# Start addresses of TensorE's operands in SBUF: streamed operands at 192 bytes past a multiple of 256, stationary ones at a multiple of 256

## The chip, the core and the metric

One core of one Trainium2 chip. The metric is device time in microseconds (us) for one execution of the whole program; the kernel before takes 1875.76 us (median of 3 runs, 1871.45 to 1876.39).

## The reference

Two blocks on 256 tokens of width 1024, all in float32. The first block has two layers; each layer is a gated feed-forward (width 2816), a mixer (a gated spatial unit beside differential attention, merged by gates), and another gated feed-forward, each followed by a layer norm:

```python
h = _swiglu(x, ffn_w1[l, 0], ffn_w3[l, 0], ffn_w2[l, 0])
x = _layernorm(ALPHA * x + 0.5 * h, ln_g[l, 0], ln_b[l, 0])
h = _mixer(x, l, w_in[l], gate_b[l], ...)
x = _layernorm(ALPHA * x + h, ln_g[l, 1], ln_b[l, 1])
h = _swiglu(x, ffn_w1[l, 1], ffn_w3[l, 1], ffn_w2[l, 1])
x = _layernorm(ALPHA * x + 0.5 * h, ln_g[l, 2], ln_b[l, 2])
```

The second block has one layer: neighbourhood attention and gated linear attention side by side, gates, an output projection, and a last gated feed-forward. Nearly all arithmetic is in the products of the activations with the weight matrices.

## The kernel before

**Products in three parts.** A weight matrix comes from HBM in chunks of 1 MB into one of three buffers `raw`. A chunk is cut into parts of 128 x 1024 numbers. For each part ScalarE writes a rounded copy `whi` (line 1371) and VectorE the remainder `wlo` (line 1835; a few times GpSimd), in four buffers of each, used in turn (`n % 4`). Activations are kept in the same two pieces, as `XTh` and `XTl`, `HCh` and `HCl`, or `ffn1Hh` and `ffn1Hl`. A product is then three matmuls: high by high, high by low, low by high.

**Two forms.** TensorE holds one operand in the array (the stationary one, 128 x 128, loaded by an LDWEIGHTS of its own for each matmul) and streams the other past it.
- `gemm_a` (lines 685, 686, 688): the weights stand, the activations stream, 256 columns. A part gives 8 x 3 = 24 matmuls. Used by all `ffn_up` stages (44 parts, 1056 matmuls each), by the mixer's q, k, u and gate projections (40 parts, 960 matmuls a layer), by its two branch projections (16 parts, 384 matmuls a layer), and by most of the second block.
- `gemm_b` (lines 708, 710, 711): the activations stand, the weights stream, 512 columns. Used by `ffn_down` (264 matmuls each), by the mixer's v, val and out projections (96 each), and by parts of the second block.

**Order.** Each engine runs a list written out by hand; they meet only through semaphores. TensorE goes through the stages in the order of the reference. Between the weight parts of the mixer, small matmuls are put in: a permutation after each q or k part (line 867), and attention steps after each gate part. In `ffn_up` up to two short modulation steps (lines 766, 768, 786) are put in. After each stage of the first block a layer norm turns the activations into `XTh` and `XTl` (TensorE line 746, ScalarE line 1379, VectorE line 1844).

**Where the operands begin.** A partition of SBUF holds the buffers one after another, so each start follows from the sizes. All of `raw`, `whi` and `wlo` begin at multiples of 512 bytes. `HCh` and `HCl` begin at a multiple of 256. The buffers of `XT` and of the feed-forward's hidden values are 512 bytes larger than needed, and the offset at which they are used differs by stage (in bytes, for the high and the low piece; the rooms themselves begin at multiples of 512):

```python
X_AT = ((256, 256), (128, 128), (64, 64), (192, 192), (384, 384), (64, 320))
H_AT = ((256, 256), (128, 128), (64, 64), (256, 0), (448, 448))
```

`X_AT` goes by stage: entries 0 and 3 are the first `ffn_up` of layers 0 and 1, entries 1 and 4 their mixers, entries 2 and 5 their second `ffn_up`. `H_AT` goes by feed-forward: four in the first block, where the hidden values stand in `ffn_down`, and the last one in the second block (`ffn4`), where they stream through `gemm_a`. So within one execution the same loops run over operands at different offsets:

| stage | us from start | streams | stands | streamed begins past 256 | standing begins past 256 |
|---|---|---|---|---|---|
| ffn_up 0 | 11 to 143 | XT | weights | 0 | 0 |
| ffn_up 1 | 486 to 614 | XT | weights | 64 | 0 |
| ffn_up 2 | 688 to 816 | XT | weights | 192 | 0 |
| ffn_up 3 | 1162 to 1290 | XT | weights | 64 | 0 |
| mixers, q k u gates | 239 to 403, 915 to 1079 | XT | weights | 128 | 0 |
| mixers, branches | 403 to 451, 1079 to 1127 | HC | weights | 0 | 0 |
| ffn_down 0, 1, 2, 3 | 143, 615, 817, 1291 | weights | hidden | 0 | 0, 128, 64, 0 |
| mixers, v, val, out | 218, 319, 452 and on | weights | XT | 0 | 128 |
| second block, forms a | 1500 to 1683 | HC | weights | 0 | 0 |
| last ffn_up | 1683 to 1803 | HC | weights | 0 | 0 |
| last ffn_down | 1803 to 1860 | hidden | weights | 192 | 0 |

**Small buffers that the change touches.** `csil` (64 bytes a partition) lies before `HCh`. In the second block `ones` is a matrix of ones for a column sum (line 1285), filled by GpSimd at line 2511; `rb` holds the reciprocal root of the last norm; `nm` is a mask that GpSimd reads at lines 2549 and 2552 for the attention bias; `c2` is a table of the linear attention.

Of the kernel before, what the change touches and what calls it, by code (L numbers as in the profile page):

```python
# [9 lines left out]
F32R = mybir.dt.float32r  # L10
# [4 lines left out]
D = 1024  # L15
T = 256
# [257 lines left out]
X_AT = ((256, 256), (128, 128), (64, 64), (192, 192), (384, 384), (64, 320))  # L274
H_AT = ((256, 256), (128, 128), (64, 64), (256, 0), (448, 448))
# [79 lines left out]
def program(nc, I, out):  # L355
# [5 lines left out]
    def shifted(stack, name, n):  # L361

        room = sb(stack, name, [128, n * T + 128], F32R)
        return lambda by: room[:, by // 4:by // 4 + n * T].rearrange("p (k c) -> p k c", k=n)
# [7 lines left out]
    with ctx:  # L372
# [27 lines left out]
        whi = some(ctx, "whi", 4, [128, 1024], F32R)  # L400
        wlo = some(ctx, "wlo", 4, [128, 1024], F32R)
# [3 lines left out]
        csil = sb(ctx, "csil", [128, 8, 2])  # L405
# [4 lines left out]
        sh = sb(ctx, "sh", [128, 48, 2])  # L410
        g1c = sb(ctx, "g1c", [128, 8, 2])
# [3 lines left out]
        sb(ctx, "gap0", [128, 80])  # L415
# [8 lines left out]
        XH, XL = [room_h(h) for h, _ in X_AT], [room_l(l) for _, l in X_AT]  # L424
# [8 lines left out]
        def ffn_bufs(st, name, *at):  # L433
            hh, hl = shifted(st, name + "Hh", NF), shifted(st, name + "Hl", NF)
            S, Hf = some(st, name + "S", 2, [128, T]), some(st, name + "Hf", 2, [128, T])
            return [(hh(h), hl(l), S, Hf) for h, l in at]


        with ExitStack() as st:
            ffn1 = ffn_bufs(st, "ffn1", *H_AT[0:3])  # L440
# [23 lines left out]
        with ExitStack() as st:  # L464
            ffn3 = ffn_bufs(st, "ffn3", H_AT[3])
# [5 lines left out]
        ones = sb(st, "ones", [128, 128])  # L471
        rb = sb(st, "rb", [128, T])
# [6 lines left out]
        nm = sb(st, "nm", [128, 2, 64])  # L479
        OGh, OGl = HCh[:, 0:4, T:512], HCl[:, 0:4, T:512]  # L480
# [26 lines left out]
        with ExitStack() as fs:  # L507
            sb(fs, "gap2", [128, 128])
            ffn4 = ffn_bufs(fs, "ffn4", H_AT[4])
            OUT = sb(fs, "OUT", [128, 2, D])  # L510
        st.close()
        FFN = [*ffn1, *ffn3, *ffn4]
# [13 lines left out]
        def hi_part(n):  # L526
            a, b = chunks[parts[n][0]][3][parts[n][1]][2:]
            return whi[n % 4][:, 0:a * b].rearrange("p (k c) -> p k c", k=a)

        def lo_part(n):  # L530
            a, b = chunks[parts[n][0]][3][parts[n][1]][2:]
            return wlo[n % 4][:, 0:a * b].rearrange("p (k c) -> p k c", k=a)
# [134 lines left out]
        def tensor(e):  # L667
# [66 lines left out]
            def xt(s):  # L734
                return lambda k: (XH[s][:, k, :], XL[s][:, k, :])

            def xt_b(s):
                return lambda k, t: (XH[s][:, k, t * 128:(t + 1) * 128], XL[s][:, k, t * 128:(t + 1) * 128])
# [103 lines left out]
            def mixer(l):  # L842
# [16 lines left out]
                gemm_b(("V", l), 8, 1, xt_b(s), (0, 1), [[4, 5], [6, 7]], 1024, lambda k, t: ready(k, (t,)), tail=3, between=turn_ws)  # L859
# [11 lines left out]
                for n in range(16):  # L871
                    b = n % 4
                    empty(b)
                    gemm_a(bank[b][:, 0:T], xt(s), ("qk", l, n), ready=ready if n == 0 else None)
# [14 lines left out]
                for n in range(8):  # L889
                    b = n % 4  # L890
                    empty(b)
                    gemm_a(bank[b][:, 0:T], xt(s), ("u", l, n))
# [3 lines left out]
                gemm_b(("val", l), 8, 1, xt_b(s), (0, 1), [[4, 5], [6, 7]], 1024, tail=2)  # L896
# [51 lines left out]
                for n in range(16):  # L948
                    b = n % 3
                    empty(b)  # L950
                    gemm_a(bank[b][:, 0:T], xt(s), ("gate", l, n))
# [24 lines left out]
                gemm_b(("out", l), 8, 1, xt_b(s), (0, 1), [[4, 5], [6, 7]], 1024, m_ready)  # L976
# [21 lines left out]
            def second():  # L998
# [281 lines left out]
                def add_square(k):  # L1280
# [4 lines left out]
                    e.matmul(bank[5][:, 0:T], ones[:, :], tmp[t2r.slot["sq", k]][:, :], start=k == 0, stop=k == 7).then_inc(  # L1285
# [63 lines left out]
            for l in range(2):  # L1349
# [3 lines left out]
                ffn_up(2 * l, xt(3 * l), x_ready(3 * l), at)  # L1353
# [4 lines left out]
                ffn_up(2 * l + 1, xt(3 * l + 2), x_ready(3 * l + 2), ffn_mods(2 * l + 1))  # L1358
# [5 lines left out]
        def scalar(e):  # L1364
# [10 lines left out]
            def turn_x(s, t):  # L1375
                for c in range(2):
                    b = (0, 1, 2, 0)[2 * t + c]
                    q.wait_ge(TURN, ("x", s, t, c))
                    e.activation(XH[s][:, 4 * c:4 * c + 4, t * 128:(t + 1) * 128], bank[b][:, :].rearrange("p (k c) -> p k c", k=4),
# [63 lines left out]
            def mixer(l):  # L1443
# [97 lines left out]
                for n in range(8):  # L1541
                    w.pass_by(1)
                    if n:
                        high("m", XH[3 * l + 1], n - 1, mtmp[tm[l].slot["m", n - 1]], ("m", l, n - 1))
                high("m", XH[3 * l + 1], 7, mtmp[tm[l].slot["m", 7]], ("m", l, 7))
# [23 lines left out]
            def second():  # L1569
# [214 lines left out]
                e.activation(rb[:, :], rb[:, :], ACTF.Sqrt).then_inc(A2.did("root"), 1)  # L1784
# [42 lines left out]
        def vector(e):  # L1827
# [11 lines left out]
            def turn_x(s, t):  # L1839
                for c in range(2):  # L1840
                    b = (0, 1, 2, 0)[2 * t + c]
                    hi = XH[s][:, 4 * c:4 * c + 4, t * 128:(t + 1) * 128]
                    q.wait_ge(XHI, ("x", s, t, c))
                    e.tensor_tensor(XL[s][:, 4 * c:4 * c + 4, t * 128:(t + 1) * 128], bank[b][:, :].rearrange("p (k c) -> p k c", k=4),  # L1844
# [72 lines left out]
            def mixer(l):  # L1917
# [122 lines left out]
                for n in range(8):  # L2040
# [6 lines left out]
                    if n:  # L2047
                        low("m", XL[3 * l + 1], XH[3 * l + 1], n - 1, mtmp[tm[l].slot["m", n - 1]])
                low("m", XL[3 * l + 1], XH[3 * l + 1], 7, mtmp[tm[l].slot["m", 7]])
# [47 lines left out]
            def second():  # L2097
# [232 lines left out]
                e.tensor_scalar(rb[:, :], bank[5][:, 0:T], 1.0 / D, RMS_EPS, ALU.mult, ALU.add).then_inc(D2.did("ms"), 1)  # L2330
                q.wait_ge(A2, "root")
                e.reciprocal(rb[:, :], rb[:, :]).then_inc(D2.did("rb"), 1)
# [315 lines left out]
```

## Time and profile before

| | |
|---|---|
| runs | 1871.45, 1875.76, 1876.39 us |
| the profiled execution | 1871.84 us, of which the span from first to last instruction is 1870.1 us |
| granted TensorE clock, mean | 0.994 of 2.4 GHz |
| TensorE matmuls | 1841.4 us busy, 98% of the span, 12859 instructions |
| TensorE weight loads | 1651.1 us, 88% |
| VectorE, ScalarE, GpSimd | 60%, 48%, 13% |
| DMA | 330.58 MB, mean 177 GB/s |

Matmuls overlap: one lasts longer than the distance to the start of the next. The time that a row of matmuls takes is therefore the number of them times the spacing of their starts. In a stretch without interruption the spacing is the length of the window, plus the duration of one matmul that overlaps its edges, over the count.

### The profile page before, as it was taken

Reading aid. Unit: us, or ns where it says so; the run is one execution under the profiler, and the core shown is the slowest. Engines: PE = TensorE matmul, PEld = TensorE weight load, DVE = VectorE, ACT = ScalarE, POOL = GpSimd, SP = SyncE. Lnnn points to the kernel's source line nnn. Section 1 sums busy time; section 2 is a strip of 40 time slices with the busy share of each in tenths; the row PEclk is TensorE's granted clock in tenths of the full one; section 3 lists DMA queues with packets and bytes.
Section 4 is the critical chain, followed back from the end, with each engine's and each line's share of the span. In section 5 each row is a group of like instructions: output and inputs, shape, how many; then the busy total and the mean of one; then the engine's idle time right before and its main releaser. Section 6 shows DMA issues by size and latency. Waiting matters only on the chain.

```text
span 1870.1 us, 31147 instructions
## 1 busy us (share of the span) xinstructions
PE 1841.4 (98%) x12859; PEld 1651.1 (88%) x12859; DVE 1125.8 (60%) x1703; ACT 890.3 (48%) x1437; POOL 245.6 (13%) x261
## 2 busy tenths in 40 slices
PE   9999999999999999999999999999998999999999
PEld 8998799999899879986898997999776787879999
DVE  5554676676656466655675776565653645565553
ACT  5544344664455435543435653555344345444443
POOL 1000232111200020001221212000111712100000
PEclk9999999999999999999999999999998999999999
DMA  8565654445666566764745455665444223356553
GB/s 277 187 203 192 232 187 155 162 136 183 203 192 211 196 209 182 243 207 157 251 158 180 136 170 191 226 209 185 170 129 131 90 77 105 113 160 191 186 182 117
DMA packets 252397, 330.58 MB, mean 177 GB/s; under 512 B 13162, under 2 KB 213072, under 8 KB 252256
## 3 DMA queue, kind: packets, MB, share of 16 engines
q1 hardware_dynamic: 248240, 315.31, 51.8%
q0 software_dynamic: 4016, 13.27, 2.0%
q8 instruction: 102, 1.67, 0.4%
q14 instruction: 39, 0.32, 0.1%
HBM read 327.51 MB, written 1.05 MB: 176 GB/s over the span
## 4 chain that ended last, share of the span: by engine, by line
PE 67%; issue 23%; DVE 5%; POOL 2%; ACT 2%; SPq 1%; DMA 1%; DVEq 0%; POOLq 0%; ACTq 0%
PE bank L685 15%; PE bank L688 15%; PE bank L686 15%; PE bank L708 5%; PE bank L710 5%; PE bank L711 5%; DVE X L1907 1%; DVE wlo L1835 1%; PE bank L1241 1%; SPq L654 1%; DMA raw<-in_w_in_dram 1%; ACT whi L1371 1%; POOL rs L2430 1%; PE bank L1219 1%; PE bank L867 1%
## 5 line engine op out<-in xcount | busy, mean ns | idle before, releaser
L1835 DVE TENSOR_TENSOR wlo<-raw,whi 128x1024 fp32r<-128x1024 f32 (+1 forms) x557 | 688.0, 1241 | 418.3 <-ACT whi L1371 415.2
L1371 ACT ACTIVATE whi<-raw 128x1024 fp32r<-128x1024 f32 (+1 forms) x569 | 594.4, 1051 | 425.3 <-PE bank L688 178.9
L685 PE MATMUL bank<-XTh,whi 128*128 128x256 f32 x2048 | 583.3, 285 | 2.8 <-DVE XTl L1844 2.8
L688 PE MATMUL bank<-XTh,wlo 128*128 128x256 f32 x2048 | 573.9, 280 | 0.0
L686 PE MATMUL bank<-XTl,whi 128*128 128x256 f32 x2048 | 573.7, 280 | 0.0
L685 PEld LDWEIGHTS bank<-XTh,whi 128*128 128x128 f32 x2048 | 386.1, 189 | 7.9 <-DVE XTl L1844 3.5
L686 PEld LDWEIGHTS bank<-XTl,whi 128*128 128x128 f32 x2048 | 386.4, 189 | 1.4
L688 PEld LDWEIGHTS bank<-XTh,wlo 128*128 128x128 f32 x2048 | 386.3, 189 | 0.0
L685 PE MATMUL bank<-HCh,whi 128*128 128x256 f32 (+1 forms) x936 | 274.1, 293 | 8.0 <-ACT whi L1371 5.9
L688 PE MATMUL bank<-HCh,wlo 128*128 128x256 f32 (+1 forms) x936 | 269.1, 287 | 0.0
L686 PE MATMUL bank<-HCl,whi 128*128 128x256 f32 (+1 forms) x936 | 269.0, 287 | 0.0
L685 PEld LDWEIGHTS bank<-HCh,whi 128*128 128x128 f32 x936 | 179.8, 192 | 26.3 <-issue 12.3
L688 PEld LDWEIGHTS bank<-HCh,wlo 128*128 128x128 f32 x936 | 179.6, 192 | 2.7 <-DVE wlo L1835 0.8
L686 PEld LDWEIGHTS bank<-HCl,whi 128*128 128x128 f32 x936 | 179.7, 192 | 2.1
L2430 POOL TENSOR_TENSOR rs<-rs,half 128x1 f32<-128x1 f32 x12 | 18.3, 1525 | 668.7 <-DVE rs L1901 668.7
L710 PE MATMUL bank<-wlo,ffn1Hh 128*128 128x512 f32 x264 | 103.8, 393 | 0.0
L708 PE MATMUL bank<-whi,ffn1Hh 128*128 128x512 f32 x264 | 103.8, 393 | 0.0
L711 PE MATMUL bank<-whi,ffn1Hl 128*128 128x512 f32 x264 | 103.7, 393 | 0.0
L708 PE MATMUL bank<-whi,XTh 128*128 128x512 f32 x192 | 77.2, 402 | 0.0
L711 PE MATMUL bank<-whi,XTl 128*128 128x512 f32 x192 | 77.1, 402 | 0.0
L710 PE MATMUL bank<-wlo,XTh 128*128 128x512 f32 x192 | 77.0, 401 | 0.0
L1403 ACT ACTIVATE ffn1S<-bank 128x256 f32<-128x256 f32 x66 | 25.4, 384 | 72.4 <-PE bank L688 72.4
(329 smaller groups left out, 2338.3 us busy)
## 6 DMA issues: line engine op xcount, KB each, us to landing
raw<-in_ffn_w_dram SPq DMA_DIRECT2D x131, 1024.0 KB, 5.1
raw<-in_w_in_dram SPq DMA_DIRECT2D x76, 1024.0 KB, 5.0
raw<-in_w_mod_dram SPq DMA_DIRECT2D x24, 1024.0 KB, 5.1
raw<-in_w_branch_dram SPq DMA_DIRECT2D x16, 1024.0 KB, 5.0
raw<-in_w_out_dram SPq DMA_DIRECT2D x12, 1024.0 KB, 5.0
raw<-in_w_ffn_gate_dram SPq DMA_DIRECT2D x11, 1024.0 KB, 5.1
raw<-in_w_ffn_up_dram SPq DMA_DIRECT2D x11, 1024.0 KB, 5.1
raw<-in_w_ffn_down_dram SPq DMA_DIRECT2D x8, 1024.0 KB, 5.0
```

Source lines behind the costliest of these rows:

```text
L654: e.dma_start(BT[64 * j:64 * j + 64, h, :, :], src).then_inc(BIAS[h].did(h, by=16), 16)
L685: e.matmul(o, hi[:, k, w0:w0 + nc_], xh, start=first and k == 0, stop=False)
L686: e.matmul(o, hi[:, k, w0:w0 + nc_], xl, start=False, stop=False)
L688: m = e.matmul(o, lo[:, k, w0:w0 + nc_], xh, start=False, stop=last and k == nk - 1)
L708: e.matmul(o[:, :], xh, hi[:, k, s], start=kk == 0, stop=False)
L710: e.matmul(o[:, :], xh, lo[:, k, s], start=False, stop=False)
L711: m = e.matmul(o[:, :], xl, hi[:, k, s], start=False, stop=kk == nparts * nk - 1)
L867: e.matmul(bank[b][:, 0:T], perm, mtmp[tm[l].slot["s", n]][:, :], start=True, stop=True).then_inc(SMALL.did(("perm", l, n)), 1)
L1371: e.activation(hi_part(n), raw_part(n), ACTF.Copy).then_inc(WHI.did(n), 1)
L1403: e.activation(S[s][:, :], bank[b][:, 0:T], ACTF.Silu).then_inc(AFF.did(("s", i, k)), 1)
L1835: e.tensor_tensor(lo_part(n), raw_part(n), hi_part(n).bitcast(F32), ALU.subtract).then_inc(WLO.did(n), 1)
L2430: e.tensor_tensor(rs[:, t, 1:2], rs[:, t, 0:1], nhalf, ALU.pow).then_inc(PLN.did(("rs", j, t)), 1)
```

## The change

Every operand of `gemm_a` and `gemm_b` that streams begins at 192 bytes (`MOVES`, 48 numbers) past a multiple of 256: `XT` in all stages, `HC` (by moving the 64 bytes of `csil` from before it to behind), the hidden values of the last feed-forward, and the weights `whi` and `wlo` in parts of 512 columns or more. Hidden values of the first block, the merged values `MX` of the mixer, and the weights in narrower parts begin at a multiple of 256 (`STANDS`). The buffers of `whi` and `wlo` grow by 256 bytes each, so the second and the fourth of each begin at 256 past a multiple of 512. `XT` as the stationary operand of the v and val projections, and `HC` as that of the second block, stay at 192. To make room, `ones` is laid over `nm` and `rb` over `c2`; the fill of `ones` on GpSimd moves behind the last use of `nm`, with a wait for it.

```diff
-X_AT = ((256, 256), (128, 128), (64, 64), (192, 192), (384, 384), (64, 320))
-H_AT = ((256, 256), (128, 128), (64, 64), (256, 0), (448, 448))
+MOVES, STANDS = 48, 0
...
-        whi = some(ctx, "whi", 4, [128, 1024], F32R)
-        wlo = some(ctx, "wlo", 4, [128, 1024], F32R)
+        whi = some(ctx, "whi", 4, [128, 1024 + 64], F32R)
+        wlo = some(ctx, "wlo", 4, [128, 1024 + 64], F32R)
...
-        csil = sb(ctx, "csil", [128, 8, 2])
         HCh = sb(ctx, "HCh", [128, 8, 512], F32R)
         HCl = sb(ctx, "HCl", [128, 8, 512], F32R)
...
+        csil = sb(ctx, "csil", [128, 8, 2])
...
-        XH, XL = [room_h(h) for h, _ in X_AT], [room_l(l) for _, l in X_AT]
+        XTh, XTl, MXh, MXl = room_h(MOVES), room_l(MOVES), room_h(STANDS), room_l(STANDS)
...
-            ffn1 = ffn_bufs(st, "ffn1", *H_AT[0:3])
+            ffn1 = ffn_bufs(st, "ffn1")
...
-            ffn3 = ffn_bufs(st, "ffn3", H_AT[3])
+            ffn3 = ffn_bufs(st, "ffn3")
...
-        ones = sb(st, "ones", [128, 128])
-        rb = sb(st, "rb", [128, T])
+        rb = c2[:, 0:T]
...
+        ones = nm[:, :, :].rearrange("p a c -> p (a c)")
...
-            ffn4 = ffn_bufs(fs, "ffn4", H_AT[4])
+            ffn4 = ffn_bufs(fs, "ffn4", MOVES)
...
         def hi_part(n):
             a, b = chunks[parts[n][0]][3][parts[n][1]][2:]
-            return whi[n % 4][:, 0:a * b].rearrange("p (k c) -> p k c", k=a)
+            at = MOVES if b >= 512 else STANDS
+            return whi[n % 4][:, at:at + a * b].rearrange("p (k c) -> p k c", k=a)
...
-                e.memset(ones[:, :], 1.0).then_inc(P2.did("ones"), 1)
...
+                q.wait_ge(P2, ("bias", 7))
+                e.memset(ones, 1.0).then_inc(P2.did("ones"), 1)
```

`lo_part` changes as `hi_part` does. No instruction is added or removed, and no shape changes.

## Rows read from the trace of the kernel before

**Rows 1.** The page: busy time of each engine; TensorE's granted clock in 40 slices.

```profile
PE 1841.4 (98%) x12859; PEld 1651.1 (88%) x12859; DVE 1125.8 (60%) x1703; ACT 890.3 (48%) x1437; POOL 245.6 (13%) x261
PEclk9999999999999999999999999999998999999999
```

**Rows 2.** Waits of TensorE: line, releaser, us in total, times, longest.

```profile
PE bank L685 <- ACT whi L1371: 5.9, 1, 5.9
PE bank L710 <- DVE wlo L1835: 4.0, 2, 3.3
```

**Rows 3.** Windows in three ffn_up stages: length, matmul busy (count), clock, DMA share, GB/s.

```profile
20.00:56.00 36.00, 36.00 (x303) 1.00 0.67 214
500.00:536.00 36.00, 36.00 (x308) 1.00 0.57 177
700.00:736.00 36.00, 36.00 (x320) 1.00 0.60 183
```

**Rows 4.** Line 686 in two of them: ns min/median/max, first and last start.

```profile
L686 PE MATMUL bank<-XTl,whi x101: 283/283/283, 19.9 to 55.9; 128*128 128x256 f32 x101
L686 PE MATMUL bank<-XTl,whi x106: 276/276/276, 700.0 to 735.7; 128*128 128x256 f32 x106
```

**Rows 5.** The same in the mixer, its branches and the last ffn_up.

```profile
L686 PE MATMUL bank<-XTl,whi x189: 274/281/287, 239.9 to 318.7; 128*128 128x256 f32 x189
L686 PE MATMUL bank<-HCl,whi x126: 278/283/283, 403.2 to 450.8; 128*128 128x256 f32 x126
L686 PE MATMUL bank<-HCl,whi x101: 283/283/283, 1699.9 to 1735.9; 128*128 128x256 f32 x101
```

**Rows 6.** The same in two stretches of the last ffn_down.

```profile
L686 PE MATMUL bank<-ffn4Hl,whi x35: 281/281/281, 1825.8 to 1837.8; 128*128 128x256 f32 x35
L686 PE MATMUL bank<-ffn4Hl,whi x37: 276/276/276, 1841.8 to 1854.0; 128*128 128x256 f32 x37
```

**Rows 7.** Windows in two ffn_down stages, columns as in Rows 3.

```profile
150.00:200.00 50.00, 50.00 (x222) 1.00 0.59 201
820.00:870.00 50.00, 50.00 (x216) 1.00 0.57 190
```

**Rows 8.** Line 711 in ffn_down 0, the val projection and ffn_down 2.

```profile
L711 PE MATMUL bank<-whi,ffn1Hl x74: 389/389/389, 149.7 to 199.4; 128*128 128x512 f32 x74
L711 PE MATMUL bank<-whi,XTl x18: 390/393/404, 323.9 to 335.8; 128*128 128x512 f32 x18
L711 PE MATMUL bank<-whi,ffn1Hl x72: 393/396/398, 820.0 to 869.7; 128*128 128x512 f32 x72
```

**Rows 9.** Groups of matmuls by shape: one of each form's three lines.

```profile
L686 PE MATMUL bank<-XTl,whi 128*128 128x256 f32 x2048 | 573.7, 280 | 0.0
L686 PE MATMUL bank<-HCl,whi 128*128 128x256 f32 x912 | 257.9, 283 | 0.0
L686 PE MATMUL bank<-ffn4Hl,whi 128*128 128x256 f32 x176 | 49.0, 278 | 0.0
L711 PE MATMUL bank<-whi,ffn1Hl 128*128 128x512 f32 x264 | 103.7, 393 | 0.0
L711 PE MATMUL bank<-whi,XTl 128*128 128x512 f32 x192 | 77.1, 402 | 0.0
L711 PE MATMUL bank<-whi,HCl 128*128 128x512 f32 x112 | 44.5, 397 | 0.0
L711 PE MATMUL bank<-whi,ffn3Hl 128*128 128x512 f32 x88 | 34.3, 390 | 0.0
```

**Rows 10.** VectorE's writes of XTl ahead of ffn_up 0 and of ffn_up 2.

```profile
L1844 DVE TENSOR_TENSOR XTl<-bank,XTh x4: 681/682/693, 7.4 to 10.6; 128x512 fp32r<-128x512 f32 x4
L1844 DVE TENSOR_TENSOR XTl<-bank,XTh x4: 681/684/693, 685.0 to 687.1; 128x512 fp32r<-128x512 f32 x4
```

**Rows 11.** Timeline of GpSimd: start, us; the fill of ones, and line 2558.

```profile
1392.18 0.22 POOL L2511 MEMSET ones<- 128x128 f32 x1
1497.21 0.72 POOL L2558 TENSOR_TENSOR ATG<-spare 128x256 f32<-128x256 f32 x1 [0.97 <-DVE spare L2208]
```

More of the change, by code:

```diff
@@ L361, in shifted @@
     def shifted(stack, name, n):
-        room = sb(stack, name, [128, n * T + 128], F32R)
-        return lambda by: room[:, by // 4:by // 4 + n * T].rearrange("p (k c) -> p k c", k=n)
+        room = sb(stack, name, [128, n * T + 64], F32R)
+        return lambda by: room[:, by:by + n * T].rearrange("p (k c) -> p k c", k=n)
     def some(stack, name, n, shape, dt=F32):
@@ L431, in program, with ffn_bufs @@
         cm, cos, sin, perm = csa[:, 0:256], csa[:, 256:512], csa[:, 512:768], csa[:, 768:896]
[L433 to L436, printed above, removed]
+        def ffn_bufs(st, name, at=STANDS):
+            return (shifted(st, name + "Hh", NF)(at), shifted(st, name + "Hl", NF)(at),
+                    some(st, name + "S", 2, [128, T]), some(st, name + "Hf", 2, [128, T]))
         with ExitStack() as st:
-            ffn1 = ffn_bufs(st, "ffn1", *H_AT[0:3])
+            ffn1 = ffn_bufs(st, "ffn1")
         with ExitStack() as st:
@@ L732, in gemm_b, with xt, xt_b, mx_b @@
                         between()
[L734 to L738, printed above, removed]
+            def xt(k):
+                return XTh[:, k, :], XTl[:, k, :]
+            def xt_b(k, t):
+                return XTh[:, k, t * 128:(t + 1) * 128], XTl[:, k, t * 128:(t + 1) * 128]
+            def mx_b(k, t):
+                return MXh[:, k, t * 128:(t + 1) * 128], MXl[:, k, t * 128:(t + 1) * 128]
             def turn_x(s, t):
@@ L895, in mixer @@
                         rotate(15)
-                gemm_b(("val", l), 8, 1, xt_b(s), (0, 1), [[4, 5], [6, 7]], 1024, tail=2)
+                gemm_b(("val", l), 8, 1, xt_b, (0, 1), [[4, 5], [6, 7]], 1024, tail=2)
                 for b in range(4, 8):
@@ L975, in m_ready @@
                     q.wait_ge(XLO, ("m", l, k))
-                gemm_b(("out", l), 8, 1, xt_b(s), (0, 1), [[4, 5], [6, 7]], 1024, m_ready)
+                gemm_b(("out", l), 8, 1, mx_b, (0, 1), [[4, 5], [6, 7]], 1024, m_ready)
             def context():
@@ L1284, in add_square @@
                         empty(5)
-                    e.matmul(bank[5][:, 0:T], ones[:, :], tmp[t2r.slot["sq", k]][:, :], start=k == 0, stop=k == 7).then_inc(
+                    e.matmul(bank[5][:, 0:T], ones, tmp[t2r.slot["sq", k]][:, :], start=k == 0, stop=k == 7).then_inc(
                         SMALL.did(("sq", k)), 1)
@@ L1352, in tensor @@
                     at[6] = turn_rows
-                ffn_up(2 * l, xt(3 * l), x_ready(3 * l), at)
+                ffn_up(2 * l, xt, x_ready(3 * l), at)
                 ffn_down(2 * l)
@@ L1357, in tensor @@
                 layernorm(3 * l + 1, (2, 8)[l])
-                ffn_up(2 * l + 1, xt(3 * l + 2), x_ready(3 * l + 2), ffn_mods(2 * l + 1))
+                ffn_up(2 * l + 1, xt, x_ready(3 * l + 2), ffn_mods(2 * l + 1))
                 ffn_down(2 * l + 1, context() if l else None)
```

38 lines of the change are left out of this document (19 added, 19 removed).

## The prediction

> **What bounds the kernel now.** The page first: TensorE's matmuls are busy for 98% of the span, the next engine for 60%, and the granted clock is at its upper level of 2.4 GHz nearly throughout [rows 1]. Then the waits: the longest that TensorE has for a split weight come to 5.9 and 4.0 us [rows 2]. So the time is a count of matmuls times the spacing of their starts, and an edit that touches only addresses can act only through that spacing. The kernel happens to run the same loop at different start offsets, so its own trace holds the comparison. ffn_up 0, 1 and 2 do the same work with the streamed activations 0, 64 and 192 bytes past a multiple of 256. In windows of 36 us they start 303, 308 and 320 matmuls [rows 3]. With one duration for the edges that is (36 + 0.283)/303 = 119.7, 117.8 and 113.4 ns each; I take 120.0 for the first, from its rows of starts. Streaming 256 columns at 2.4 GHz takes 106.7 ns, so 13.3 ns of loss at offset 0 have become 6.7 ns at 192. The duration of one follows: 283 ns at the first, 276 at the third, every one of them alike [rows 4]. Duration less 163 ns is the spacing, and I use that where interruptions spoil a count.
>
> **Form a, part by part** (counts are three times those of [rows 9], by stage as the loops give them).
> - ffn_up 0: 1056 matmuls from 120.0 to 113.4 ns: 7.0 us. ffn_up 1 and 3: 2112 from 117.8 to 113.4: 9.3 us. ffn_up 2 is at 192 already: 0. The last ffn_up, at offset 0, lasts 283 ns each, so 120 [rows 5]: 1056 by 6.6 is 7.0 us. These run with few interruptions, as ffn_up 2 does, and its rows are the price.
> - Stages with many interruptions have a second price. The last ffn_down streams at 192 too, and one of its stretches has 281 ns (118 ns apart), another 276 (113 apart), each of them constant, with four transposes between [rows 6]. So at 192 TensorE can fall into a slower rhythm and keep it until the next interruption. Bounds for the mixers and the second block are 113.4 and 117.8. I take 114.5, one restart in four slow, since ffn_up 2 comes back to 276 after its own. The mixers' q, k, u and gates stream at offset 128 with a median of 281 but a scatter of 274 to 287 [rows 5]; the distances of their starts average 118.8: 1920 by 4.3 is 8.3 us (1.9 to 10.4). Their branches are at 283, so 120 [rows 5]: 768 by 5.5 is 4.2 us (1.7 to 5.1). The rest of the second block, 912 matmuls: 5.0 us (2.0 to 6.0).
> - The last ffn_down keeps offset and rhythm: 0, give or take 1.
> Form a comes to 40.8 us, with 28.9 and 44.8 as ends.
>
> **Form b** has never streamed at anything but offset 0 in this trace; only the standing operand moved. ffn_down 0, both at 0: 222 starts in 50 us, (50 + 0.389)/222 = 226.9 ns, which is 213.3 for 512 columns plus 13.6; ffn_down 2, standing at 64: 216, or 233.3 ns [rows 7]. The durations agree, 389 and 396; the val projection, standing at 128, has a median of 393 and reaches 404 [rows 8], 232.4 ns on average. The price of streaming at 192 is thus unknown, and bounded by rows. The low end is 220: form a loses 13.3 ns at offset 0, form b 13.6, the same loss though it streams twice as long, and form a's shrinks by 6.6 at 192. The high end is 233.3: at standing 64 and streaming 0 the streamed operand begins 192 ahead of the standing one modulo 256, exactly the distance that the change makes. I take 220, for that equality of the two losses says that they arise in the same first part of a matmul, while the weights load. Counts again by [rows 9]:
> - ffn_down 0 and 3, 528 by 6.7: 3.6 us. ffn_down 1 (standing at 128, 232.4): 264 by 12.4, 3.3 us. ffn_down 2: 264 by 13.3, 3.5 us. out, where MX stands at 0: 192 by 12.4, 2.4 us.
> - v and val: XT stands at 192 and the weights stream at 192. Equal offsets exist only as 0 and 0, so 226.7 (220 to 233): 384 by 5.7, 2.2 us. HC in the second block goes from equal to equal, 0 (gain of 2.3 to loss of 2.2).
> Form b comes to 15.0 us, with a gain of 19.8 and a loss of 1.7 as ends.
>
> **The rest.** The writers' cost does not hang on the offset: VectorE writes XTl in 682 ns at offset 0 and in 684 at 192 [rows 10]. The modulation's 80 matmuls also stream at 192, under 1 us either way. Feeding: ffn_up 2 already ran at the new spacing with DMA at 183 GB/s in a window in which ffn_up 0 drew 214 [rows 3], and without a wait that lists among the longest [rows 2], so splits and loads can follow in the other stages. The fill of ones (0.22 us) moves behind GpSimd's last bias step, with a wait for its own predecessor. Queued behind it is line 2558, which sat idle for 0.97 us waiting for VectorE [rows 11]: that idle time covers it, and without it the sums for the linear attention, and TensorE behind them, would be those 0.22 us and the wait later. The reader of ones, line 1285, comes stages later. rb over c2 costs nothing: c2 has long been read.
>
> **A rule against it.** The rows show 120 and 113.4 ns for the same instruction at two addresses [rows 3]. The Trainium skill, TensorE: Matmul & The Clock Gate, Back-to-back issue gap, gives a gap that depends on the columns alone, and SBUF — State Buffer, Who interferes with whom, gives TensorE two independent read ports for the two operands. By both there is nothing to gain. The trace disagrees with the first by its number; of the second it shows only that the weight load and the stream together lose more or less by address. That result is rival 3 below.
>
> **The sum.** 40.8 + 15.0 = 55.8 us off the profiled execution of 1871.8 gives 1816.0. That execution is 3.9 us under the median of the runs, so I forecast 1820.
>
> **The rivals.**
> 1. *Only the distance between the two start offsets counts.* Then form b gets 233.3 in ffn_down and out: 528 by +6.6, 264 by +0.9 and 192 by +0.9 are a loss of 3.9, v and val still gain 2.2. For it: form b's worst row has this distance. Against it: the equal losses above. Gain 40.8 - 1.7 = 39.1: 1837.
> 2. *The slow rhythm is the rule.* The buffers' new stride or the restarts put TensorE at 118 in all of form a, ffn_up 2 with it: 2.3 + 0 + 2.3 + 5.6 - 4.6 = 5.6, and form b 4.4 above 220 where it streams at 192 against 0, 15.0 - 5.5 = 9.5. Total 15: 1861. For it [rows 6], against it the whole of ffn_up 2.
> 3. *The address is not the cause*, and ffn_up 2 is faster for some other reason of its own, so the change does not do what it says: 1876. Against it: three offsets, three spacings, and 281 or 276 only where the offset is 192.
> 4. *Slower.* Two of four standing weight buffers now begin at 256 past a multiple of 512. If the read pattern repeats over 512 bytes on the standing side, every second part meets a conflict. The price by form b's worst loss, 20 ns over the stream, is 106.7 + 20 = 126.7 for half of form a's 9408 matmuls, mean 120.0 against 118.2 now: +17, less 6 from form b at an unchanged 226.7, 1887. It decides from about 124 ns in the odd buffers. Against it: ffn_down 0 stands at 256 past 512 and ffn_down 3's low piece at 0, with 389 and 390 ns [rows 8, 9].
>
> **How the numbers follow.** Forecast 0.48, rival 1 0.33, rival 2 0.10, rival 3 0.05, rival 4 0.04. The predicted time is the forecast's, 1820. The forecast's own range, from the ends of the unknown prices, is 1811 (gain 65) to 1849 (gain 27), and holds rival 1. With some room for the scatter of the runs I give 1808 to 1850. About 0.3% is what a measurement can tell from no change: faster 0.92, same 0.04, slower 0.04.
>
> **What would show it.** Right: line 686 at 276 ns in every ffn_up, a 36 us window with 320 matmuls; line 711 at about 382 in ffn_down. Rival 1 shows as 396 there, rival 2 as 281 in line 686 over whole stages, rival 4 as two durations that alternate with the weight buffer. The prediction is wrong if TensorE's waits for `whi` or `wlo` grow past some 20 us, or if the mixers stay at 281.

## The result, and the profile after

| | before | after |
|---|---|---|
| runs, us | 1871.45, 1872.81, 1875.76, 1876.39 | 1837.98, 1841.89, 1842.32, 1847.04 |
| median | 1874.28 | 1842.11 |
| ratio | | 0.983, 95% interval 0.9802 to 0.9859 |
| profiled execution, its span | 1871.8, 1870.1 | 1842.3, 1840.6 |

A fourth run of the kernel before, 1872.81 us, came with the result and moves its median to 1874.28. The change takes 32 us off; 55.8 were forecast. The profiled executions differ by 29.5 us, in the span as in the time. The page of after, then its waits of TensorE (line, releaser, us in total, times, longest):

```profile
PE 1807.9 (98%) x12859; PEld 1615.1 (88%) x12859; DVE 1123.9 (61%) x1703; ACT 891.9 (48%) x1437; POOL 247.1 (13%) x261
PEclk9999999999999999999999999999998999999999
```

```profile
PE bank L684 <- ACT whi L1373: 6.2, 1, 6.2
PE bank L709 <- DVE wlo L1837: 4.1, 2, 3.4
```

The same number of matmuls, TensorE as full as before, and the two longest waits as they were [rows 1, 2]: splits and loads did follow, and nothing took TensorE's place as the bound. The gain is in the spacing. Windows of after in ffn_up 0, ffn_up 1, the last ffn_up, ffn_down 0 and ffn_down 2 (length, matmul busy and count, clock, DMA share, GB/s):

```profile
20.00:56.00 36.00, 36.00 (x319) 1.00 0.74 239
500.00:536.00 36.00, 36.00 (x320) 1.00 0.58 178
1690.00:1726.00 36.00, 36.00 (x320) 1.00 0.59 184
145.00:190.00 45.00, 45.00 (x195) 1.00 0.55 187
815.00:860.00 45.00, 45.00 (x194) 1.00 0.55 189
```

Where [rows 3] had 303 and 308 matmuls in 36 us there are now 319 and 320, that is 113.4 ns each, in every ffn_up. ffn_down has (45 + 0.396)/194.5 = 233.4 ns in both stages, where [rows 7] gave 226.9 for ffn_down 0. The matmuls themselves (lines are one lower than before in `gemm_a` and `gemm_b`; ns min/median/max): line 685 in ffn_up 0, the mixer's q, k, u parts, its gate parts, the neighbourhood attention and the last ffn_up, then line 710 in ffn_down 0 and the val projection.

```profile
L685 PE MATMUL bank<-XTl,whi x106: 276/276/279, 19.8 to 55.7; 128*128 128x256 f32 x106
L685 PE MATMUL bank<-XTl,whi x175: 276/281/282, 239.6 to 312.2; 128*128 128x256 f32 x175
L685 PE MATMUL bank<-XTl,whi x109: 276/276/282, 340.0 to 391.9; 128*128 128x256 f32 x109
L685 PE MATMUL bank<-HCl,whi x180: 276/281/281, 1479.8 to 1599.1; 128*128 128x256 f32 x180
L685 PE MATMUL bank<-HCl,whi x107: 276/276/276, 1679.8 to 1715.9; 128*128 128x256 f32 x107
...
L710 PE MATMUL bank<-whi,ffn1Hl x65: 393/393/398, 145.1 to 189.9; 128*128 128x512 f32 x65
L710 PE MATMUL bank<-whi,XTl x12: 389/389/389, 323.8 to 331.3; 128*128 128x512 f32 x12
```

Two durations, 276 and 281, now make up nearly all of form a (113.3 and 117.8 ns apart), where [rows 4, 5] had 283 and a scatter round 281. The long stretches have 276, the fast rhythm; the q, k, u parts and the attention have a median of 281, the slow one. In form b ffn_down lost its 389 [rows 8], and val got 389 for 393. The groups of line 685 and 710:

```profile
L685 PE MATMUL bank<-XTl,whi 128*128 128x256 f32 x2048 | 567.2, 277 | 0.0
L685 PE MATMUL bank<-HCl,whi 128*128 128x256 f32 x912 | 253.5, 278 | 0.0
L710 PE MATMUL bank<-whi,ffn1Hl 128*128 128x512 f32 x264 | 104.4, 395 | 0.0
L710 PE MATMUL bank<-whi,XTl 128*128 128x512 f32 x192 | 75.1, 391 | 0.0
```

Against [rows 9], form a is 3 to 5 ns shorter each, ffn_down 2 ns longer, and the projections from XT 11 ns shorter. Of these 11, some 7 are no effect of the addresses: in before's profile the first matmuls of both v projections were granted the lower clock of 1.2 GHz and last 628 ns, in after's profile none of them. Windows of before at the two places (columns as above):

```profile
214.60:218.00 3.40, 3.40 (x10) 0.51 1.02 416
890.50:893.90 3.40, 3.40 (x10) 0.50 1.03 414
```

In the stretches without interruption v and val went from 232.4 to 226.7, and out from 232.4 to 233.3.

**Where the 29.5 us are.** The length of each stage, from the start of its first to that of its last matmul of that form in the two traces, with the forecast beside it (us, gain positive; the second block's form a with HC stands in two stretches, and the row of its form b holds the first of them too):

| stages | length before | after | gain | forecast |
|---|---|---|---|---|
| ffn_up 0 | 131.7 | 124.7 | 6.9 | 7.0 |
| ffn_up 1 and 3 | 129.3, 129.3 | 124.6, 124.6 | 9.3 | 9.3 |
| ffn_up 2 | 129.5 | 129.5 | 0.0 | 0 |
| last ffn_up | 128.3 | 121.5 | 6.8 | 7.0 |
| mixers, q k u gates | 80.1, 60.8, 80.3, 60.8 | 79.3, 59.9, 79.3, 59.8 | 3.8 | 8.3 |
| mixers, branches | 48.6, 48.6 | 46.7, 46.7 | 3.8 | 4.2 |
| second block, other forms a | 5.6, 165.2 | 5.5, 165.1 | 0.2 | 5.0 |
| last ffn_down (to 1865.5 in before) | 62.0 | 62.0 | 0.0 | 0 |
| ffn_down 0 and 3 | 59.6, 61.6 | 61.4, 63.1 | -3.2 | 3.6 |
| ffn_down 1 | 61.1 | 61.4 | -0.3 | 3.3 |
| ffn_down 2 | 61.4 | 61.4 | 0.0 | 3.5 |
| out | 22.1, 22.1 | 22.2, 22.2 | -0.2 | 2.4 |
| v and val | 24.6, 22.1, 24.6, 22.1 | 23.9, 21.6, 23.5, 21.6 | 2.9 | 2.2 |
| HC, form b | 140.8 | 141.4 | -0.7 | 0 |

The gains sum to 29.3; the rest is rounding and the gaps between stages. Of the 26.5 us that the forecast had too much, 16.5 are form b (15.0 against -1.5) and 10 are form a (40.8 against 30.8), nearly all of these in the mixers and the second block.

Two rows hold the clock beside the addresses. In v the lower clock cost before's profile some 1.5 us at the start of each projection (the first ten intervals take 3.98 us, against 2.42 and 2.41 in after); 2.2 of these 3.1 us were not missed, as the one long pause in each was 1.0 us in before and 2.3 and 1.9 in after, so that some 0.9 of the 2.9 us are not the change's. In the second block the same 72 matmuls of form b with HC took 21.6 us in before and 22.9 in after, at equal spacing but with more of the stretch at the lower clock (window, matmul busy and count, clock, DMA share, GB/s; before, then after):

```profile
1451.50:1473.10 21.60, 18.25 (x74) 0.92 0.37 109
1427.80:1450.70 22.90, 19.52 (x73) 0.85 0.35 106
```

That row's loss of 0.7 is thus no sign of a price of the new addresses.

### The profile page after: what moved, and what is told of

It is laid out like the page before. It is cut to its first block, busy times and chain, and to the rows that moved or that the text cites. A ratio compares the mean times of both kernels' runs of the same rounds, so it can differ in the third digit from the quotient of the medians.

```text
span 1840.6 us, 31147 instructions
## 1 busy us (share of the span) xinstructions
PE 1807.9 (98%) x12859; PEld 1615.1 (88%) x12859; DVE 1123.9 (61%) x1703; ACT 891.9 (48%) x1437; POOL 247.1 (13%) x261
## 4 chain that ended last, share of the span: by engine, by line
PE 63%; issue 23%; DVE 6%; DMA 3%; POOL 2%; ACT 2%; SPq 1%; DVEq 0%; POOLq 0%; ACTq 0%
PE bank L684 15%; PE bank L687 14%; PE bank L685 14%; PE bank L707 4%; PE bank L709 4%; PE bank L710 4%; DMA G<-in_lam_dram 1%; DVE X L1909 1%; DVE wlo L1837 1%; PE bank L1243 1%; SPq L653 1%; DMA raw<-in_w_in_dram 1%; POOL rs L2432 1%; ACT whi L1373 1%; PE bank L1221 1%
## 5 line engine op out<-in xcount | busy, mean ns | idle before, releaser
L684 PE MATMUL bank<-XTh,whi 128*128 128x256 f32 x2048 | 576.8, 282 | 2.0 <-DVE XTl L1846 2.0
L685 PE MATMUL bank<-XTl,whi 128*128 128x256 f32 x2048 | 567.2, 277 | 0.0
L687 PE MATMUL bank<-XTh,wlo 128*128 128x256 f32 x2048 | 567.1, 277 | 0.0
L684 PE MATMUL bank<-HCh,whi 128*128 128x256 f32 (+1 forms) x936 | 270.0, 288 | 8.9 <-ACT whi L1373 6.2
L685 PE MATMUL bank<-HCl,whi 128*128 128x256 f32 (+1 forms) x936 | 264.7, 283 | 0.0
L687 PE MATMUL bank<-HCh,wlo 128*128 128x256 f32 (+1 forms) x936 | 264.5, 283 | 0.0
L710 PEld LDWEIGHTS bank<-whi,ffn1Hl 128*128 128x128 f32 x264 | 49.6, 188 | 12.0
```

Source lines behind the costliest of these rows:

```text
L684: e.matmul(o, hi[:, k, w0:w0 + nc_], xh, start=first and k == 0, stop=False)
L685: e.matmul(o, hi[:, k, w0:w0 + nc_], xl, start=False, stop=False)
L687: m = e.matmul(o, lo[:, k, w0:w0 + nc_], xh, start=False, stop=last and k == nk - 1)
L710: m = e.matmul(o[:, :], xl, hi[:, k, s], start=False, stop=kk == nparts * nk - 1)
```

## The experiments

Two questions: what in the addresses sets the spacing, the offset of each operand or the distance between them (streamed start minus standing start, modulo 256, below "the distance"), and what decides between 276 and 281 ns.

**Only the distance kept.** Streamed operands at a multiple of 256, standing ones at 64 past one; `csil` goes back before `HC`.

```diff
-MOVES, STANDS = 48, 0
+MOVES, STANDS = 64, 16
```

> Both operands of every matmul of the two forms begin 64 bytes further than in the changed kernel: streamed ones at 0 past a multiple of 256, standing ones at 64 (XT and HC, where they stand, at 0), so the distance from standing to streamed start stays what it was. If only the distance counts: form a at 276 to 281 ns in the same places, form b at 393 to 398 in ffn_down and 389 in val, time within 0.3% of the changed kernel, about 1842. If the streamed operand's own offset counts: form a at 283 everywhere (spacing 120, plus some 52 us), form b at 389 in ffn_down (less 8), about 1886.

Measured: 1844.61 us (1838.86 to 1848.32), ratio to before 0.9856, interval 0.9832 to 0.988: overlapping that of after. Windows in ffn_up 0, ffn_up 1 and ffn_down 0, columns as above:

```profile
20.00:56.00 36.00, 36.00 (x308) 1.00 0.67 220
500.00:536.00 36.00, 36.00 (x321) 1.00 0.61 197
145.00:190.00 45.00, 45.00 (x194) 1.00 0.57 200
```

ffn_up 1 streams at a multiple of 256 and has the fast spacing, (36 + 0.276)/321 = 113.0; before, streaming at 0 with the weights at 0 too, ffn_up 0 had 120. ffn_down has its 233.3 again. So it is the distance that sets the spacing, and neither operand's own offset. The 308 in ffn_up 0 is the slow rhythm (281 ns) in its first 623 matmuls; the rest have 276.

**Distance 0 everywhere**, with all of the change's other moves (the wider weight buffers, `ones` over `nm`); `csil` goes back before `HC` here too.

```diff
-MOVES, STANDS = 48, 0
+MOVES, STANDS = 0, 0
```

> Every operand of the two forms begins at a multiple of 256, all else as in the changed kernel. Form a back to 120 ns from 113.4 to 117.8 (plus some 52 us), form b from 233.3 to 226.7 in ffn_down and out (1248 matmuls, less 8.2): 1886, slower than the kernel before by 0.6%. If instead the wider weight buffers or the moved fill of ones made the gain, it stays near 1842.

Measured: 1883.4 us (1882.71 to 1885.77), ratio 1.007, interval 1.0053 to 1.0087. Windows in ffn_up 0, ffn_up 2 and ffn_down 0:

```profile
20.00:56.00 36.00, 36.00 (x303) 1.00 0.69 218
700.00:736.00 36.00, 36.00 (x302) 1.00 0.59 187
145.00:190.00 45.00, 45.00 (x201) 1.00 0.56 187
```

All of form a at 120 ns, ffn_up 2 too, which had 113.4 before; all of form b at 226.7. Nothing but the distance gives the gain. This kernel and the changed one lie 41 us apart by two constants and the place of `csil`.

**The weights stream at 0.** As after, but in form b the weights begin at a multiple of 256, as the hidden values do.

```diff
         def hi_part(n):
...
-            at = MOVES if b >= 512 else STANDS
+            at = STANDS
```

> Only form b's weights go back to streaming at 0; form a as in the changed kernel. Distance theory: ffn_down and out have distance 0 again, 389 ns (226.7 apart), less 8.2 us; v, val and the second block's form b get distance 64, which no run has shown yet, 226 to 236 apart (720 matmuls, 0 to plus 6 us). Time 1834 to 1840. Rival, form b's loss is not from the addresses: 396 ns stays, 1842.

Measured: 1838.38 us (1835.08 to 1844.89), ratio 0.983, interval 0.9805 to 0.9855. Window in ffn_down 0, then line 710's group from XT, then line 685 in ffn_up 0 and in ffn_up 1:

```profile
145.00:190.00 45.00, 45.00 (x201) 1.00 0.58 192
```

```profile
L710 PE MATMUL bank<-whi,XTl 128*128 128x512 f32 x192 | 75.5, 393 | 0.0
```

```profile
L685 PE MATMUL bank<-XTl,whi x106: 276/276/281, 20.0 to 55.8; 128*128 128x256 f32 x106
L685 PE MATMUL bank<-XTl,whi x103: 281/281/281, 490.0 to 526.0; 128*128 128x256 f32 x103
```

Form b is decided by this: at distance 0 ffn_down has 226.7 ns again (its four stages together 6.7 us shorter than after's), and v and val, at distance 64, have 229.0 and 233.4 in place of 227.4 and 226.9. But the whole gained only what the runs can't separate. In the profiled execution ffn_up 1, at unchanged addresses, ran its first 623 matmuls in the slow rhythm and the last ffn_up nearly all of its own: 2.8 and 4.5 us longer than in after. The time of form b is settled, that of the kernel has a second cause.

**A scan of distances.** The kernel before has a table of offsets by stage, so one kernel tries six distances in form a and five in form b. Three such tables were run, the third with different distances for the high and the low piece:

```diff
-X_AT = ((256, 256), (128, 128), (64, 64), (192, 192), (384, 384), (64, 320))
-H_AT = ((256, 256), (128, 128), (64, 64), (256, 0), (448, 448))
+X_AT = ((224, 224), (240, 240), (208, 208), (176, 176), (160, 160), (32, 32))
+H_AT = ((240, 240), (224, 224), (192, 192), (208, 208), (480, 480))
...
+X_AT = ((200, 200), (196, 196), (184, 184), (48, 48), (188, 188), (16, 16))
+H_AT = ((16, 16), (32, 32), (48, 48), (96, 96), (452, 452))
...
+X_AT = ((192, 0), (192, 208), (192, 128), (208, 192), (192, 64), (192, 32))
+H_AT = ((80, 80), (112, 112), (144, 144), (0, 16), (448, 384))
```

> The kernel before with other offsets by stage, to read the spacing at distances between the multiples of 64: form a in ffn_up 0, 1, 2, 3 at 224, 208, 176, 32, in the mixers at 240 and 160; form b in ffn_down 0, 1, 2, 3 with standing offsets 240, 224, 192, 208 (distance 16, 32, 64, 48), in the mixers at distance 16 and 96. If steps of 64 bytes count, 208 to 240 behave like 192 (276 ns or 281), 160 and 176 like 128 (281 with scatter), 32 like 0 (283). If each 16 bytes count, the durations change gradually, and one of 208, 224 or 240 may be under 276. The total is not of interest; near 1865.

> The kernel before with offsets by stage again: form a in ffn_up 0, 1, 2, 3 at distance 200, 184, 48, 16, in the mixers at 196 and 188, the last ffn_down at 196; form b in ffn_down 0, 1, 2, 3 at distance 240, 224, 208, 160, in the mixers at 60 and 68. If the two rhythms at 192 (276 and 281 ns) are special to that distance, 188 and 196 show a single one between them, near 279; if one of them shows 276 after every interruption of the mixer, it is the better offset. For form b none is expected under 389 ns (distance 0).

> The kernel before with the high and low piece of XT at different offsets: 192 and 0 in ffn_up 0, 192 and 208 in mixer 0, 192 and 128 in ffn_up 1, 208 and 192 in ffn_up 2, 192 and 64 in mixer 1, 192 and 32 in ffn_up 3. If each matmul pays only by its own distance, the three in a row (two on the high piece, one on the low) average to a third of one and two thirds of the other: with 113.4 or 117.8 at 192 and 120 at 0, 116 to 118.5 in ffn_up 0. If the rhythm is a matter of the whole cycle, one pair may hold 113 to 115 after every interruption of a mixer, which would be a way to be rid of the slow one.

Measured: 1871.63, 1888.82 and 1880.85 us, one run each. Windows of the first table in ffn_up 0, 1 and 2 (distances 224, 208, 176); of the second in ffn_up 0 and 1 (200, 184); of the third in ffn_up 0 (192 with 0):

```profile
20.00:56.00 36.00, 36.00 (x307) 1.00 0.68 219
500.00:536.00 36.00, 36.00 (x311) 1.00 0.61 194
700.00:736.00 36.00, 36.00 (x305) 1.00 0.59 186
```

```profile
20.00:56.00 36.00, 36.00 (x302) 1.00 0.65 218
500.00:536.00 36.00, 36.00 (x303) 1.00 0.58 188
```

```profile
20.00:56.00 36.00, 36.00 (x308) 1.00 0.67 222
```

The window's length plus one duration, over the count, gives 118.2, 116.7, 119.0, 120.2, 119.7 and 117.8 ns. From the starts in all traces, means over stretches without interruption (ns; the third table's kernel only where both pieces have one distance):

| distance | 0 | 16 | 32 | 48 | 64 | 112 | 128 | 160 | 176 | 184 | 188 | 192 | 196 | 200 | 208 | 224 | 240 |
|---|---|---|---|---|---|---|---|---|---|---|---|---|---|---|---|---|---|
| form a | 120.0 | 118.4 | 116.7 | 118.3 | 117.8 | | 118.8 | 117.8 | 119.3 | 120.0 | 118.4 | 113.3 or 117.8 | 121.7 | 120.0 | 116.9 | 118.3 | 117.2 |
| form b | 226.7 | 228.3 | 233.3 | 232.0 | 228.9 or 233.3 | 226.7 | 232.4 | 234.3 | 232.0 | | | 233.3 | | | 233.3 | 233.3 | 226.7 |

Steps of 64 bytes are too coarse to describe this. For form a 192 in its fast rhythm is the best of all, and a narrow one: 4 bytes to either side it is gone; in its slow rhythm 32, 208 and 240 are better. For form b 0 is as good as any, and 64 has two values as well: with the weights streaming at 0, v has 228.9 and val 233.3 at the same offsets. The two forms want different distances. The means hide some spread: at distance 128 in before, the u parts have 118.7 in layer 0 and 119.9 in layer 1, where XT begins 256 bytes further, while the q, k and gate parts are alike in both layers. ffn_up 1 and 3 of before, with the low piece at 64 and at 320, have the same 117.8, which speaks for a pattern of 256 bytes.

With the pieces apart, ffn_up 0 (192 and 0) has 118.0 throughout, and no pair of distances has less than 116.8: none keeps the fast rhythm behind every interruption.

**Each form its own distance.** Weights of the v and val projections and of the second block's form b stream at 192 against XT and HC at 192, all other weights of form b at 0 against 0, form a as after.

```diff
+        at_192 = set()
+        for c_, (src_, _, width_, hs_) in enumerate(chunks):
+            if hs_ and hs_[0][3] >= 512 and src_.tensor.name in ("in_w_in_dram", "in_w_in_2_dram"):
+                at_192.add(c_)
...
-            at = MOVES if b >= 512 else STANDS
+            at = MOVES if parts[n][0] in at_192 else STANDS
```

> The changed kernel with form b's weights at the offset of what stands beside them: 0 in ffn_down and out, 192 in v, val and in the second block. Form a keeps distance 192, form b gets 0. Distance theory: ffn_down and out at 389 ns, less 8.2 us against the changed kernel, nothing else: 1834. If the share of form a's slow rhythm differs, which I cannot foresee, up to 8 us more or less.

> The kernel of e6_each_form_its_distance once more. Its first profile had 44% of the XT matmuls in the slow rhythm, among them the first 650 of an ffn_up, which ate the 8.2 us that form b gave back. If the moment decides, long stretches of ffn_up at 276 ns and others at 281 than before, share from 15% to 50%, time 1832 to 1846. If the program decides, the same stretches at 281 ns and 1840 again.

Measured: 1841.88 us (1839.11 to 1846.4, 5 runs), ratio 0.9843, interval 0.9824 to 0.9863; the program once more, on another chip, 1845.77. Form b is at 226.7 throughout, and in the stage lengths 8.0 us shorter in ffn_down and out than after; the kernel is not faster. Line 689 (form a's second matmul here) of the first profile in ffn_up 1, 3 and the last ffn_up, then the same windows of the second profile:

```profile
L689 PE MATMUL bank<-XTl,whi x103: 281/281/281, 479.8 to 515.9; 128*128 128x256 f32 x103
L689 PE MATMUL bank<-XTl,whi x103: 281/281/281, 1149.9 to 1186.0; 128*128 128x256 f32 x103
L689 PE MATMUL bank<-HCl,whi x107: 276/276/276, 1689.8 to 1725.8; 128*128 128x256 f32 x107
```

```profile
L689 PE MATMUL bank<-XTl,whi x106: 276/276/276, 480.0 to 515.7; 128*128 128x256 f32 x106
L689 PE MATMUL bank<-XTl,whi x107: 276/276/276, 1149.9 to 1185.9; 128*128 128x256 f32 x107
L689 PE MATMUL bank<-HCl,whi x103: 281/281/281, 1689.8 to 1725.8; 128*128 128x256 f32 x103
```

One program, two executions, and the stretches of 281 ns have changed places. So the rhythm isn't set by the addresses alone. (That the chip decides is ruled out further down, where two executions on one chip differ in the same way.) Each stretch keeps the rhythm it begins with: the slow half of ffn_up 1 costs 623 x 4.4 ns = 2.8 us, the stretch of 1187 matmuls that runs from the last ffn_up into the last ffn_down 5.2 us.

The two profiles show one thing more, the granted clock at the start of ffn_up 1, in the first and in the second:

```profile
475.00:478.50 3.50, 3.48 (x29) 1.00 1.09 392
```

```profile
475.00:478.50 3.50, 3.50 (x19) 0.59 1.07 395
```

In the second TensorE came out of the layer norm, in which it runs only some transposes and a modulation step, at the lower level of 1.2 GHz, and its first matmuls started 213 ns apart: 19 in 3.5 us for 29, some 1.6 us lost. It did so at the start of three of the stages in this profile, and of none in the first.

**The weight buffers' stride.** As with the weights at 0, and `whi` and `wlo` 1024 wide again, so that all eight begin at multiples of 512.

```diff
-        whi = some(ctx, "whi", 4, [128, 1024 + 64], F32R)
-        wlo = some(ctx, "wlo", 4, [128, 1024 + 64], F32R)
+        whi = some(ctx, "whi", 4, [128, 1024], F32R)
+        wlo = some(ctx, "wlo", 4, [128, 1024], F32R)
```

> As e3_weights_stream_at_0, with whi and wlo 4096 bytes apart again instead of 4352, all starts the same past 256. If the new spacing of the buffers (half of them at 256 past a multiple of 512) brings the slow rhythm of form a, the share of 281 ns falls from e3's third to near none, the mixers come to 276, and the time to some 8 us under e3: 1830. If it has no part in it, the shares scatter as before and the time is e3's, 1838.

> The changed kernel, one more execution. If the program decides which rhythm follows an interruption, the same parts of the mixers are at 281 ns as in its first profile (one in four of the q and k parts at 276, nearly all gate parts at 276). If the moment decides, other parts are slow, and the share differs; that would be the reason why the changed kernel's runs scatter by 0.5%, from 1838 to 1847, against 0.3% before.

Measured: 1841.07 us (1836.13 to 1841.17), ratio 0.9828, interval 0.9809 to 0.9846; the changed kernel once more 1845.65. Line 685 in the narrow kernel's q, k, u parts:

```profile
L685 PE MATMUL bank<-XTl,whi x172: 276/281/283, 239.8 to 311.6; 128*128 128x256 f32 x172
```

The same median of 281 as after. Laid out part by part, both kernels show one part at 276 ns and about three parts at 281 ns in turn through the q and k parts, and nearly all gate parts at 276. The buffers turn over every four parts in both, but begin at different offsets past a multiple of 512, so neither their stride nor that offset makes the pattern: in layer 0 the narrow kernel has its fast parts one for one where the wide kernel with the weights at 0 has them. The PSUM bank written turns over every four parts too; no run separates it from the buffer's number.

The changed kernel's second profile has the same share in the q and k parts, in other places (3rd, 7th, 11th, 15th part of layer 0 in place of the 3rd, 5th, 9th, 13th), and its first branch stage mostly at 281 (305 of 384 matmuls, 25 in the first profile). So neither the program nor the moment alone decides. One profile of the nine at distance 192 stands apart: with both operands 64 bytes further, the q and k parts alternate one by one from the 3rd on, in both layers. The offsets may thus have a part in the rhythm, though not in the two spacings; one profile doesn't show it.

**An interruption early in the stage.** The kernel with a distance for each form, and the modulation steps of ffn_up 1 and 3 earlier.

```diff
-MODS = ({12: 0}, {12: 3}, {12: 5, 16: 6}, {12: 9})
+MODS = ({12: 0}, {2: 3}, {12: 5, 16: 6}, {2: 9})
```

> The kernel of e6 (form a at distance 192, form b at equal offsets), with the two modulation steps of ffn_up 1 and ffn_up 3 put after their 2nd pair of parts, in place of the 12th; the same work, the same addresses. Earlier profiles at distance 192: of 70 stretches of form a that began behind a modulation step 66 had the fast rhythm (276 ns), of 42 that began behind a form b only 12, and in e6's profile the first 623 matmuls of ffn_up 1 and of ffn_up 3 were slow, in e10's those of ffn_up 1 were not. Theory (the rhythm is drawn anew at each interruption and kept until the next): ffn_up 1 and 3 are slow for at most some 150 matmuls and fast (113.3 ns) for the other 900 each; about 1836 to 1840 us, up to 4 us less than e6's 1842, and less scatter. Rival (the rhythm belongs to the stage or to the moment and not to what went before): stretches of 281 ns as long as before, 1842 us.

> The same program once more, for a second profile. If what precedes a stretch sets its rhythm, ffn_up 1 and 3 are fast behind their modulation steps in both profiles, while the mixers and the last ffn_up may differ between the two executions. If the rhythm belongs to the moment, ffn_up 1 or 3 is slow in one of them.

Measured: 1839.03 us (1836.22 to 1844.35, 5 runs), ratio 0.9817, interval 0.9801 to 0.9833; once more, on the same chip, 1838.5. Line 689 in ffn_up 3 and the last ffn_up, first profile and second:

```profile
L689 PE MATMUL bank<-XTl,whi x92: 276/276/286, 1149.8 to 1185.7; 128*128 128x256 f32 x92
L689 PE MATMUL bank<-HCl,whi x103: 281/281/281, 1689.8 to 1725.8; 128*128 128x256 f32 x103
```

```profile
L689 PE MATMUL bank<-XTl,whi x92: 276/276/286, 1150.0 to 1185.8; 128*128 128x256 f32 x92
L689 PE MATMUL bank<-HCl,whi x106: 276/276/276, 1690.0 to 1725.7; 128*128 128x256 f32 x106
```

ffn_up 1 and 3 were fast behind their steps both times, as the theory wants, but also ahead of them, so the steps had nothing to mend and the test doesn't tell the theories apart. Pooled over the nine profiles in which form a has distance 192: of 90 stretches behind a modulation step 86 were fast, behind a form b 12 of 54, behind any other short interruption 649 of 1041. The rhythm of a stretch thus goes with what comes before it. But each kind of interruption has its own stages and places, so the counts don't tell the interruption from the place; and that it decides alone is refuted, with the last ffn_up going both ways here, in one program on one chip. The stretch before has a part: in all nine profiles the 131 matmuls behind the stretch of 1187, with four transposes between, have the other rhythm than those 1187. The interval overlaps those of after and of all kernels at distance 192: 1838 to 1845 us as medians, none of them separable from the changed kernel. No version beat it.

## Why the prediction was right, and where it was wrong

**What holds.** The bound (TensorE's spacing), that only addresses act, and that feeding follows: waits unchanged. The long stages of form a are right to 0.2 us each: 6.9, 9.3, 0.0 and 6.8 against 7.0, 9.3, 0 and 7.0. Comparing the same loop at three offsets in one trace was enough for that. Moving `ones` and `rb` cost nothing that shows: the kernel with all at 0 has them too and lies where 120 and 226.7 ns put it. The time lies in the range given, nearest to the first rival's 1837, not to the forecast's 1820. The range's upper end was drawn a little short: form b's loss of 1.7 leaves out the low ends of v, val (233) and HC (a loss of 2.2); with them it is 6.4. Nothing hangs on it here.

**The step that failed: form b at 220 ns.** It rested on "the equal losses arise in the same first part of a matmul", from 13.3 and 13.6 ns at offset 0 in the two forms. Equal losses at one distance say nothing about another: at 192, form a's loss fell to 6.6 and form b's rose to 20. The row for it was there, ffn_down 2 with distance 192 and 233.3 ns [rows 7], and the prediction named it as the high end. The first rival is what holds: only the distance counts, shown by the kernel that shifts both operands by 64 bytes (113.0 and 233.3 again). Its form b, a loss of 1.7 us, was measured as 1.5; that these agree so well is in part luck, for v holds some 0.9 us and HC 0.7 of the clock with opposite signs. A trace that has only ever moved one operand can't tell offset from distance, and then the row with the same distance is the nearest one.

**The term mis-sized: restarts.** "One restart in four slow", 114.5 ns in mixers and second block, was taken from the stage with the longest stretches. In the q, k, u parts some four matmuls in five are slow (116.9 on average), in the gates one in seven (114.2), in the second block's attention nearly all (median 281). The mixers' spacings gave 5.4 us for the 8.3 forecast, and of these 1.6 were lost again in the intervals across the interruptions, which grew; 3.8 remain. The second block gave 0.2 for 5.0, and of what is missing 1.6 us are a stretch at the lower clock in after's profile which before's doesn't have, behind three interruptions of 1.1 to 1.2 us from start to start (window, matmul busy and count, clock, DMA share, GB/s):

```profile
1620.40:1623.60 3.20, 3.19 (x16) 0.50 0.19 16
```

The mixers lie between the ends that the prediction gave (1.9 and 10.4), the second block, with those 1.6 us added back, just under its low end (1.8 for 2.0). The first rival's gain of 39.1 less 4.5 in the mixers and 4.8 in the second block is 29.8, against the 29.5 measured. So the second rival's mechanism is a part of the truth: the slow rhythm isn't the rule, but the q, k and u parts have it mostly, in every profile. Dense interruptions alone don't bring it: the gates have one after each part and are mostly fast. And the second block's attention is slow by chance in after's profile. Its 15 parts between the attention steps are all at 281 there and in three other profiles, all at 276 in the other five, so for instance in the second profile of the last kernel:

```profile
L689 PE MATMUL bank<-HCl,whi x186: 276/276/282, 1486.8 to 1599.9; 128*128 128x256 f32 x186
```

Where these parts are fast and the clock stays up behind them, as in the profile with the weights streaming at 0, the stretch of 165.2 us takes 162.2: a gain of 3.0, inside the ends that the prediction gave.

**Rivals 3 and 4** are refuted: at distance 0 everywhere the gain is gone, and wide or narrow buffers give the same time (1838.38 and 1841.07 us, their intervals overlapping). The same 256 columns took 113.3, 120.0 and 121.7 ns by address. The Trainium skill, TensorE: Matmul & The Clock Gate, Back-to-back issue gap, gives the gap by the number of columns and names no address; the traces here disagree.

## What to carry to other kernels

Where TensorE is the bound and nothing else is left, look at the start addresses of its two operands: here the distance between them modulo 256 bytes was worth 1.7% of the kernel, and the best distance differed by the number of columns streamed (192 for 256 columns, 0 for 512). Measure the spacing of starts by stage, for each form by itself, before choosing one offset for all. A gain of a few tenths of a per cent on top can't be told by one profile, when one program shows a different rhythm in each execution.

## What the runs showed of the hardware that was not expected

- The spacing follows the distance of the two start addresses modulo 256, and shifting both operands alike left it as it was: 120.0 ns at 0, 113.3 at 192, 121.7 at 196 for 256 columns; 226.7 at 0, 233.3 at 192 for 512. The one exception seen is the u parts at distance 128 (118.7 and 119.9).
- At distance 192 there are two rhythms for 256 columns, 113.3 and 117.8 ns (276 and 281 ns of duration), each kept exactly until the next interruption, up to 1187 matmuls long: of 1185 stretches of 16 and more in nine profiles none changes midway. The same program has them in other places in another execution; the share of matmuls at 281 ns went from 19% to 40% of form a over nine profiles, and each 10% of form a's some 9,400 matmuls is 4 us. Form b has two values at distance 64 (228.9 and 233.3 ns), which no run followed up. The runs of the kernels at 192 lie 0.3 to 0.5% apart, those with distance 0 everywhere 0.2%; but the kernel before, with little work at 192, has 0.4% over nine runs, so that the rhythms are the cause is argued, not shown.
- After a layer norm, or a row of short waits in the second block, TensorE's next matmuls were granted the lower clock in some executions (0.50 to 0.59 in the windows above): 213 ns apart in place of 113 to 120 for 256 columns, 427 in place of 227 to 232 for 512, some 1.6 us each. Beside the stretches at the lower clock that every profile has in the second block, between 1388 and 1475 us, it happened twice in before's profile (at both v), once in after's, three times in the second profile of the kernel with a distance for each form, five times in the first of the last kernel. No run here tells why in one and not in another. Two profiles can differ by several us in this alone, which is as much as form b was worth.
